# Gate and up sums in two halves of a bank: one double-width matmul for the high weight part, joined later, and ten coarser row classes

## The reference

```python
logits = xf @ w_router + b_router
top_logit, top_e = lax.top_k(logits, 4)
gates = jax.nn.softmax(top_logit, axis=-1)
hu = lax.ragged_dot(xs, w_gate_up, group_sizes) + b_gate_up[e_sorted]   # rows sorted by expert
gate = jnp.minimum(hu[:, :1024], 7.0)
up = jnp.clip(hu[:, 1024:], -7.0, 7.0)
act = (up + 1.0) * gate * jax.nn.sigmoid(1.702 * gate)
y = lax.ragged_dot(act, w_down, group_sizes) + b_down[e_sorted]
```

## Time and profile before

| | us |
|---|---|
| median of 3 runs | 4533.25 |
| lowest and highest run | 4527.98, 4533.9 |
| profiled execution, first to last instruction (its span) | 4529.3 |
| TensorE busy in it | 4289.9 |
| VectorE busy in it | 3076.1 |
| ScalarE busy in it | 1817.6 |
| GpSimd busy in it | 1010.1 |

### The profile page before, as it was taken

The page is one execution under the profiler, slowest core; times in us unless marked ns, Lnnn a source line. Parts: engine busy times, 40 slices in busy tenths (PEclk is TensorE's granted clock), DMA queues, the critical chain, the costliest instruction groups (busy, mean ns, idle before and its releaser), DMA issues. The chain is left out here.

```text
span 4529.3 us, 70549 instructions
## 1 busy us (share of the span) xinstructions
PE 4289.9 (95%) x24356; PEld 3153.5 (70%) x24356; DVE 3076.1 (68%) x4861; ACT 1817.6 (40%) x2677; POOL 1010.1 (22%) x1152
## 2 busy tenths in 40 slices
PE   8999988999999998699999999999999999999987
PEld 4444434444444454599989889899999999999961
DVE  2587867878888873555556556666676777777768
ACT  1222223443434433233434444444445555555530
POOL 1111101221111122211112212222222222222235
PEclk9999989999999999799999999999999999999986
DMA  6443330120110010544555456474657667667668
GB/s 194 126 122 92 87 101 16 30 27 21 18 23 16 14 27 19 148 158 148 174 168 190 155 183 220 162 250 161 237 197 239 208 230 241 219 234 237 212 214 362
DMA packets 534140, 665.72 MB, mean 147 GB/s; under 512 B 64416, under 2 KB 402592, under 8 KB 533952
## 3 DMA queue, kind: packets, MB, share of 16 engines
q1 hardware_dynamic: 419664, 501.02, 34.7%
q10 hardware_dynamic: 87744, 77.15, 5.4%
q0 software_dynamic: 26576, 85.56, 5.0%
HBM read 543.61 MB, written 120.03 MB: 147 GB/s over the span
## 5 line engine op out<-in xcount | busy, mean ns | idle before, releaser
L2000 PE MATMUL gu<-x_hi,w_hi 128*128 128x240 f32 (+8 forms) x4096 | 1196.5, 292 | 4.1 <-issue 4.1
L2003 PE MATMUL gu<-x_lo,w_hi 128*128 128x240 f32 (+8 forms) x4096 | 1195.5, 292 | 0.5 <-issue 0.5
L2004 PE MATMUL gu<-x_hi,w_lo 128*128 128x240 f32 (+8 forms) x4096 | 1194.1, 292 | 0.0
L2106 DVE TENSOR_TENSOR w_lo<-w_raw,w_hi 128x2048 fp32r<-128x2048 f32 x386 | 874.6, 2287 | 414.1 <-ACT w_hi L2190 386.2
L2190 ACT ACTIVATE w_hi<-w_raw 128x2048 fp32r<-128x2048 f32 x386 | 726.8, 1908 | 207.4 <-PE gu L2004 132.0
L2000 PEld LDWEIGHTS gu<-x_hi,w_hi 128*128 128x128 f32 x4096 | 774.7, 189 | 4.5 <-issue 4.3
L2003 PEld LDWEIGHTS gu<-x_lo,w_hi 128*128 128x128 f32 x4096 | 773.3, 189 | 1.1 <-issue 0.9
L2004 PEld LDWEIGHTS gu<-x_hi,w_lo 128*128 128x128 f32 x4096 | 773.8, 189 | 0.0
L1972 POOL TENSOR_TENSOR a_lo<-up,a_hi 128x384 fp32r<-128x384 f32 x256 | 396.6, 1549 | 1177.8 <-ACT a_hi L2202 1177.8
L570 PE MATMUL proj_acc<-w_in_sb,hT 128*128 128x512 f32 (+1 forms) x1280 | 499.0, 537 | 0.7 <-ACT hT L586 0.7
L2000 PE MATMUL yp<-w_hi,a_hi 128*128 128x512 f32 x1088 | 445.6, 410 | 2.3
(11 more groups left out here) (316 smaller groups left out, 5878.6 us busy)
## 6 DMA issues: line engine op xcount, KB each, us to landing
w_raw<-w_gate_up SPq DMA_DIRECT2D x258, 1024.0 KB, 7.6
w_raw<-w_down SPq DMA_DIRECT2D x128, 1024.0 KB, 8.1
y_dram<-y_rows ACTq DMA_DIRECT2D x128, 256.0 KB, 2.6
y_dram<-zeros ACTq DMA_DIRECT2D x12, 2688.0 KB, 15.5
h_blk<-h_dram SPq DMA_DIRECT2D x32, 512.0 KB, 8.7
qi_dram<-qi_stage ACTq DMA_DIRECT2D x16, 640.0 KB, 3.2
x_in<-x SPq DMA_DIRECT2D x16, 512.0 KB, 6.1
w_in_sb<-w_in SPq DMA_DIRECT2D x4, 2048.0 KB, 14.2
```

Of the source, the lines that this page charges most:

```text
L2000: op = nc.tensor.matmul(out, s_hi_, m_hi, start=(n == 0), stop=False)
L2003: nc.tensor.matmul(out, s_hi_, m_lo, start=False, stop=False)
L2004: op = nc.tensor.matmul(out, s_lo_, m_hi, start=False, stop=(n == len(pairs) - 1))
L2106: nc.vector.tensor_tensor(w_lo[:, c % 2, cols], raw[:, c % 3, cols], w_hi[:, c % 2, cols].bitcast(F32), ALU.subtract).then_inc(s_lo, 1)
```

## The change

The classes are no longer an even ladder. `WIDTHS` is ten widths, 384, 352, 320, 304, 288, 272, 256, 240, 208 and 176. A visit in a class of at most 256 ("parted") makes its gate and up sums another way: a bank of 512 columns is taken as two sums of 256. One matmul sends w_hi over x_hi and x_lo, which now lie in one tensor, side by side: twice the width, into both sums. A second one sends w_lo over x_hi into the first sum. ScalarE copies the second sum to SBUF, and VectorE joins both with the bias. All element work of a parted visit is on 256 columns. GpSimd's part is as before.

```diff
-WIDTHS = tuple(range(ROWS, 2 * P - 17, -GRAIN))
+WIDTHS = (384, 352, 320, 304, 288, 272, 256, 240, 208, 176)
+KINDS = tuple((ROWS - width) // GRAIN for width in WIDTHS)
+LAST_KIND = tuple(kind - 1 for kind in KINDS[1:]) + KINDS[-1:]
+ONE_SUM = sum(width > 2 * P for width in WIDTHS)
+PEELED = 2
...
-                nc.gpsimd.iota(class_no[:], pattern=[[1, len(WIDTHS)]], base=0, channel_multiplier=0,
-                               allow_small_or_imprecise_dtypes=True).then_inc(s_made, 1)
+                for n, step, many in ((0, 2, 2), (2, 1, 5), (7, 2, 2), (9, 1, 1)):
+                    op = nc.gpsimd.iota(class_no[:, n:n + many], pattern=[[step, many]], base=LAST_KIND[n], ...)
+                op.then_inc(s_made, 1)
...
+                nc.vector.tensor_scalar(ends[:, ONE_SUM - 1:], ends[:, ONE_SUM - 1:], float(PEELED), None, ALU.max)
+                dve.drain()
...
-        x_hi = sb("x_hi", [P, KD, ROWS], F32R)
-        x_lo = sb("x_lo", [P, KD, ROWS], F32R)
+        x_both = sb("x_both", [P, 2, KD, ROWS], F32R)
+        x_hi, x_lo = x_both[:, 0], x_both[:, 1]
...
+                def two_sums(bank, width, triples):
+                    out = bank.rearrange("p (s n) -> p s n", s=2)[:, :, 0:width]
+                    for n, (w_high, w_rest, moving) in enumerate(triples):
+                        nc.tensor.matmul(out, w_high, moving, start=(n == 0), stop=False)
+                        op = nc.tensor.matmul(out[:, 0], w_rest, moving[:, 0], start=False, stop=(n == len(triples) - 1))
+                    return op
...
+                    if parted:
+                        g, u = g[:, 0:2 * P], u[:, 0:2 * P]
+                        dve.wait_ge(s_sig, 24 * v + 3 * j + 1)
+                        nc.vector.scalar_tensor_tensor(g, gu[:, j % 2, 0, 0:2 * P], b_gate, g, ALU.add, ALU.add)
+                        dve.drain()
+                        nc.vector.tensor_scalar(g, g, LIMIT, None, ALU.min).then_inc(s_gm, 1)
+                        dve.wait_ge(s_g1, 16 * v + 2 * j + 2)
+                        dve.wait_ge(s_sig, 24 * v + 3 * j + 2)
+                        nc.vector.scalar_tensor_tensor(u, gu[:, j % 2, 1, 0:2 * P], b_up, u, ALU.add, ALU.add
+                                                       ).then_inc(s_gu, 1)
+                        dve.drain()
+                        nc.vector.tensor_scalar(u, u, LIMIT, -LIMIT, ALU.min, ALU.max)
+                        dve.drain()
+                        nc.vector.scalar_tensor_tensor(u, u, 1.0, g, ALU.add, ALU.mult)
+                        return
...
+                def second_sums(v, j):
+                    act.wait_ge(s_g1, 16 * v + 2 * j + 1)
+                    nc.scalar.activation(gate[:, j % 2, 0:2 * P], gu[:, j % 2, 0, 2 * P:], ACT.Copy).then_inc(s_sig, 1)
+                    act.wait_ge(s_g1, 16 * v + 2 * j + 2)
+                    act.wait_ge(s_al, 8 * v + max(j - 1, 0))
+                    nc.scalar.activation(up[:, j % 2, 0:2 * P], gu[:, j % 2, 1, 2 * P:], ACT.Copy).then_inc(s_sig, 1)
...
                     for c in range(4):
+                        if c and parted:
+                            second_sums(v, 2 * c - 1)
                         high(v, c + 1, 0)
                         if c:
-                            sigmoid(v, 2 * c - 1)
+                            sigmoid(v, 2 * c - 1, parted)
                         high(v, c + 1, 1)
                         if c:
-                            high_act(v, 2 * c - 1)
+                            high_act(v, 2 * c - 1, parted)
                         elif not first(v):
-                            store(v - 1, 5)
-                        sigmoid(v, 2 * c)
-                        high_act(v, 2 * c)
+                            store(last, 5)
+                        if parted:
+                            second_sums(v, 2 * c)
+                        sigmoid(v, 2 * c, parted)
+                        high_act(v, 2 * c, parted)
```

More of the change, by code:

```diff
@@ L2014, in up_chunk @@
                             cols = slice(jj * P, (jj + 1) * P)
[L2015 to L2018, removed]
+                            if width <= 2 * P:
+                                op = two_sums(gu[:, jj, h], width,
+                                              [(hi[:, k, h, cols], lo[:, k, h, cols], x_both[:, :, k, 0:width])
+                                               for k in range(KD)])
+                            else:
+                                op = passes(gu[:, jj, h, 0:width],
+                                            [(hi[:, k, h, cols], lo[:, k, h, cols], x_hi[:, k, 0:width],
+                                              x_lo[:, k, 0:width]) for k in range(KD)])
+                            op.then_inc(s_g1, 1)
                 def up(v, width):
@@ L2175, in _, with high @@
                     low_x(0, k)
-                over_visits(dve, body)
+                more = dve.value_load(S["more"][0:1, 0:1], min_val=EXPERTS - 1, max_val=MAX_VISITS - 1)
+                one_sum = dve.value_load(S["ends"][0:1, ONE_SUM - 1:ONE_SUM], min_val=PEELED, max_val=MAX_VISITS - 1)
+                body(0, False)
+                with dve.Fori(1, one_sum) as v:
+                    body(v, False)
+                with dve.Fori(one_sum, more + 1) as v:
+                    body(v, True)
             @block.scalar
             def _(act):
-                def high(v, c, half):
+                def high(v, c, half, after=None):
                     n = 12 * v + 2 * c + half
@@ L2185, in high @@
                         if c >= 2 and c < 6:
-                            act.wait_ge(s_g1, 8 * v + 2 * (c - 2) + 2)
+                            act.wait_ge(s_g1, 16 * v + 4 * (c - 2) + 4)
+                        elif after is not None:
+                            act.wait_ge(s_g2, 6 * after + 3)
                         elif not first(v):
@@ L2194, in high_x, with sigmoid, high_act @@
                     nc.scalar.activation(x_hi[:, k], turned_x(v, k)[:, 0:ROWS], ACT.Copy).then_inc(s_xh, 1)
[L2196 removed]
+                def second_sums(v, j):
[4 more added lines that the diff above has]
+                    nc.scalar.activation(up[:, j % 2, 0:2 * P], gu[:, j % 2, 1, 2 * P:], ACT.Copy).then_inc(s_sig, 1)
+                def sigmoid(v, j, parted):
                     act.wait_ge(s_gm, 8 * v + j + 1)
[L2198 to L2200 removed]
+                    width = 2 * P if parted else ROWS
+                    nc.scalar.activation(sig[:, j % 2, 0:width], gate[:, j % 2, 0:width], ACT.Sigmoid, scale=SWI_ALPHA
+                                         ).then_inc(s_sig, 1 if parted else 3)
+                def high_act(v, j, parted):
                     act.wait_ge(s_act, 8 * v + j + 1)
[L2202 removed]
+                    width = 2 * P if parted else ROWS
+                    nc.scalar.activation(a_hi[:, j, 0:width], up[:, j % 2, 0:width], ACT.Copy).then_inc(s_ah, 1)
                 def store(v, n):
@@ L2248, in _ @@
                     high_x(0, k)
-                n = over_visits(act, body)
+                more = act.value_load(S["more"][0:1, 0:1], min_val=EXPERTS - 1, max_val=MAX_VISITS - 1)
+                one_sum = act.value_load(S["ends"][0:1, ONE_SUM - 1:ONE_SUM], min_val=PEELED, max_val=MAX_VISITS - 1)
+                body(0, False)
+                with act.Fori(1, one_sum) as v:
+                    body(v, False)
+                with act.Fori(one_sum - 1, more) as before:
+                    body(before + 1, True, before)
+                n = more + 1
                 store(n - 1, 5)
```

61 lines of the change are left out of this document (34 added, 27 removed).

## The result

The changed kernel takes 4548.42 us (median of 10 runs, 4541.01 to 4553.11) beside 4532.12 us for the kernel before (10 runs, 4527.65 to 4540.75): a ratio of 1.0036, 95% interval 1.0028 to 1.0044. It is slower, by 16.3 us. The forecast was 4535.8, no change; the result lies in the range of 4514 to 4560, on the side of the slower cases, but for none of the three reasons given there.

A forecast was written before the change was run, and what follows sets the result against it. TensorE bounds the kernel now; after the change VectorE's 10.90 us a chunk bounds narrow visits. Gains of 1.4 and 2.7 less 6.6 lose 2.5 us: 4533.25 + 2.5 = 4535.8 us, no change, range 4514 to 4560.

The forecast's parts named there:

- the three reasons given there: Three slower forms: join at 0.61 us (4560), clamp waiting for the rest's copy (4546), join locked out by a_lo (4596).
- What bounds it: Expert stage: TensorE bounds it, busy 99.86 of 100 us; VectorE is near, working 10.08 of every 10.87 us chunk.
- TensorE's gain: Gate and up matmuls: 0.9 us a visit at 256 and 240, 4.9 at 208, 8.6 at 176; 48.9 us if TensorE-bound.
- The classes: Coarser classes cost 6.6 us: 3.4 for 336 to 352, 2.7 for the first visit, 0.5 for the placing stage.
- VectorE's cycle: VectorE per chunk in narrow visits: 9.71 us work, 0.87 wait for ScalarE, 0.32 held by GpSimd: 10.90 us.
- The hold-up of the gate clamp: VectorE's gate clamp behind the weight residue is held by GpSimd's a_lo, 0.2 to 0.4 us, 0.25 taken.
- The sum of a visit: Twelve narrow visits: 4 x 0.03 = 0.12 us more each, tail 0.24 shorter, so 1.4 us gained in all.
- VectorE keeps up: Rival, narrow visits: VectorE's work is hidden ahead, TensorE alone bounds; 42 us gained, 4491 us; chance 0.04.
- The cycle is shorter: Rival, VectorE's chunk: no hold-up by GpSimd, 10.58 us (4522 us), or 10.32 with a 0.42 join (4515); chance 0.18.
- The slower rival: VectorE's chunk in narrow visits: a dear join or longer lock takes the cycle to 11.04 us or more; chance 0.28.
- a dear join: First join behind each weight residue: it takes 0.61 us instead of 0.485, cycle 11.40, time 4560 us.
- a longer lock: VectorE against GpSimd: clamp waits for the rest's copy (cycle 11.12, 4546 us), or a_lo locks out the join (12.17, 4596).

The follow-up runs named there:

- experiment 11: Kernel before, with GpSimd's last copy of the rest in each visit cut into 16 pieces of 4 columns; 4786.21 us, ratio 1.0567.
- the classes alone: Changed kernel keeping only its ten coarser classes: no double-width matmul, three matmuls a group, element work on 384 columns; 4528.23 us, ratio 0.9998.
- experiment 1: Changed kernel with nine throwaway 512-column matmuls before the last group of the first down tile, visits of at most 256 rows; 4545.33 us, ratio 1.0033.
- experiment 2: Changed kernel with GpSimd's a_lo cut to 256 columns and its copy of the rest left out in parted visits; 4532.64 us, ratio 0.9999.
- experiment 6: Changed kernel with the edits of experiment 2 and experiment 3 together; 4504.63 us, ratio 0.9944.
- experiment 3: Changed kernel with ScalarE's copy of the gate's second sum (tile 2c+1) ahead of the a_hi copy (tile 2c); 4519.42 us, ratio 0.9974.
- experiment 5: Changed kernel with the first two down tiles of a narrow visit interleaved, their last groups at the end; 4528.03 us, ratio 0.9995.
- experiment 9: Changed kernel with the first two down tiles interleaved and transposes of the next tokens' pieces 2 and 3 moved between; 4529.59 us, ratio 0.9999.

## Why the prediction was off

*What bounds it.* Right. TensorE is not the bound in the narrow visits, and they are equally long whatever their width, as VectorE's 10.08 of 10.87 us in the earlier trace rows suggested.

*TensorE's gain.* Right where TensorE is the bound, if a little low: 0.9 us was forecast for a visit of 256, and it is 1.6. From the first gate matmul to the first transpose behind the up sums it needs 44.89 us at 256 and 42.32 at 240, 11.22 and 10.58 a chunk, where 11.33 and 10.65 were forecast. A group takes 0.300 at 208 and 0.274 at 176 (0.301 and 0.273).

*The classes.* 6.6 us forecast. 336 to 352 costs 3.5, right; the rest is lost in what the start of the stage and its first visit vary by from run to run (1874 to 1889 us, and 104.3 to 107.9, experiment 11 left out). In the whole the classes alone give 0.9998, with some 5 us that the narrow classes gain in it.

*VectorE's cycle.* Right in its parts: joins 0.48 (0.485), the plain clamp 0.294 (0.30), products 0.425 (0.43, 0.42), the wait for ScalarE's copy 0.87 (0.87, in each chunk), `a_lo` at 2.55 us. The hold-up of the gate clamp is 0.26 (0.25 taken), that of 0.07 in odd tiles didn't come. The cycle is 10.99 where 10.90 stood; the difference lies in the steps: a join behind a clamp that isn't held starts 0.31 us after it (3646.91, 3647.22), where 0.22 was added, and the stretch with the residues takes 4.99 (3637.53 to 3642.52), where 4.93 was.

*The sum of a visit: the step that failed first.* "4 x 0.03 = 0.12 us more each", less a tail of 0.24, was to make a narrow visit 0.12 shorter; without any fall of the clock it is 0.6 longer. The first chunk doesn't follow the cycle: its even tile starts 8.05 us into the visit in both kernels, and what counts is the stretch from there to the odd tile, 3.23 us with an idle of 0.36 before and 3.70 with the new wait of 0.87 after. The cycle's other stretch, with the residues, the one that got shorter, is not in it. That makes 0.46, then 3 x 0.11, less 0.18 in the tail: 0.62. Twelve visits, each some 0.72 longer than forecast, are 8.6 us.

*The price of a wait: the step that was missing.* The prediction priced TensorE's wait at its own length. It said that TensorE would wait for GpSimd's rest; but it didn't ask what the granted clock, 1.00 from 1900 to 4380 us before (the earlier trace rows show 100 of them), does behind an idle of 2.1 to 3.3 us. It falls in eight of the twelve narrow visits, 1.56 us in seven and 2.4 in the last, 13.3 us. Experiments 1 and 11 show this from both sides.

*The two together* are 22 us over the forecast of +2.5; the greater gain at 256 (2 us) and the cheaper classes give back the rest. *The rivals.* "VectorE keeps up" was out: the narrow visits wait for it. "The cycle is shorter" was out: the hold-up by GpSimd came, and the cycle is 10.99. The slower rival had the right side with the wrong place: neither a dear join nor a longer lock. It said that a cycle of 11.04 decides; the cycle is 10.99, and it is slower all the same.

## What to carry to other kernels

When a second engine's cycle comes near the bound engine's, work out when the last piece of a round arrives, from the first chunk on and with the wait that each chunk adds; a change per cycle is not enough. Look where the lag of a round collects: one idle time on TensorE can cost its length and a fall of the clock behind it, so spreading, shortening or filling the wait pays beyond its length. And a queue order that was harmless while the engine had slack (the high part of one tile ahead of the sums of the next) is the first thing to turn round when a new wait shows at its end.

## What was not expected of the hardware

The clock. Behind idle times of TensorE of 1.2 to 1.35 us at this place it fell in none of 17 visits (experiments 1, 2 and 6), behind 2.0 to 3.3 us in 20 of 28 (the changed kernel and experiments 2, 3 and 6), behind 6.1 us in all 15 visits of 256 and 240 rows of experiment 11. It fell within the idle in experiment 11 (0.92 over the 6 us, 0.50 behind), and which visits it hits differs between equal visits of one run. Nor is the length of an idle all: behind waits of about 2 us at the transposes of experiment 5 it fell in none of seven visits of 208 and 176, and behind waits of 2.0 us for VectorE in the up part it fell in both visits of 176 of experiments 1, 5 and 9, and in one of the two of the changed kernel. These falls cost nothing that shows, since VectorE bounds the up part there: visits of 176 in experiment 5 take 68.07 us, as those of 208 do without a fall. Why the place matters is open. The Trainium skill ("TensorE: Matmul & The Clock Gate", What's actually happening) says that the throttled state is the default and that activity releases it; the granted clock here has two values, 0.50 and 1.00, with steps of 0.426 and 0.234 us, which agrees.

The lock between VectorE and GpSimd. The Trainium skill ("SBUF — State Buffer", Who interferes with whom) says that one of the two holds the shared path for a whole instruction. In experiment 11 two copies of 4 columns took 2.27 us instead of 0.185, each beside a residue of 2.29 us, which agrees. With `a_lo` on 256 columns and no copy behind it (experiment 2), it ended 0.1 us and not 0.4 into the clamp, and the clamp that met it went from 0.55 to 0.294 us, its time alone.

GpSimd's small copies. A copy of 4 columns took 0.185 us where one of 64 took 0.24 (medians of experiment 11), so cutting it makes it no shorter in proportion. The starts of the small ones lie 0.12 us apart; by that estimate sixteen would have taken the 2 us that were wanted, but they met VectorE's next two residues, and the last group came 6 us late.
